# Nine plain tiles of the first expert group before the one-hot turns instead of seven, the other seven at 14 products a turn

## The reference, cut to what matters

```python
q = jnp.einsum('bsd,de->bse', xn, w_query).reshape(B, S, PEER_HEADS, 2, PEER_HALF)
s = jnp.einsum('bshpd,hpnd->bshpn', q, sub_keys)
top_s, top_i = lax.top_k(s, PEER_TOPK)
...
expert = i1 * PEER_N_KEYS + i2
gates = jax.nn.softmax(cand_s, axis=-1)
...
a = jax.nn.gelu(jnp.einsum('cd,ced->ce', xc, u), approximate=False) * gc
return jnp.einsum('ce,ced->cd', a, vv)
```

## Time and profile before

| | us |
|---|---|
| median of 3 runs | 3599.85 |
| lowest and highest run | 3598.56, 3603.22 |
| the profiled execution's own time | 3599.3 |
| its span, first to last instruction | 3597.6 |
| mean granted TensorE clock | 0.991 of full |
| TensorE busy | 3491.2 (97%) |
| VectorE busy | 2541.8 (71%) |
| ScalarE busy | 1731.0 (48%) |
| GpSimd busy | 116.1 (3%) |

### The profile page before, as it was taken

How to read it: one execution, slowest core, us unless ns; L and a number is a source line. 1 busy time by engine, 2 the same in 40 slices (tenths; PEclk the granted TensorE clock), 3 DMA queues, 4 the chain that set the end, 5 groups by cost and what they waited for, 6 DMA issues and landing times.

```text
span 3597.6 us, 70310 instructions
## 1 busy us (share of the span) xinstructions
PE 3491.2 (97%) x27342; PEld 3337.9 (93%) x27342; DVE 2541.8 (71%) x4337; ACT 1731.0 (48%) x3177; POOL 116.1 (3%) x209
## 2 busy tenths in 40 slices
PE   6899999999999999999999999999998999999998
PEld 6898889898899999999999999988966999999998
DVE  7976535888658797878787888943356776767555
ACT  4531113546855454545445445742155655555444
POOL 0001000000100000000000000000000000000000
PEclk9999999999999999999999999999999999999999
DMA  9979876654666868687877777532211455555554
GB/s 404 406 265 366 341 280 221 252 183 152 223 252 237 315 241 313 249 303 250 303 264 298 268 282 295 197 129 88 91 45 37 172 195 193 194 191 195 177 192 161
DMA packets 118196, 829.40 MB, mean 231 GB/s; under 512 B 13104, under 2 KB 13232, under 8 KB 26800
## 3 DMA queue, kind: packets, MB, share of 16 engines
q1 hardware_dynamic: 88416, 619.20, 47.5%
q0 software_dynamic: 29520, 206.58, 15.1%
HBM read 806.86 MB, written 16.78 MB: 229 GB/s over the span
## 4 chain that ended last, share of the span: by engine, by line
PE 88%; DVE 6%; ACT 2%; DMA 2%; issue 1%; POOL 0%; SPq 0%; DVEq 0%; ACTq 0%
PE ps L1182 23%; PE ps L1184 23%; PE ps L1183 23%; PE ps L1157 9%; DVE arena L1749 2%; PE ps L1265 1%; PE ps L1267 1%; PE ps L1268 1%; ACT arena L615 1%; DVE ring_low L1739 1%; DMA gates_scratch<-arena 1%; PE ps L1581 1%; DMA gates_scratch<-cb 1%; PE ps L1209 0%; PE ps L1211 0%
## 5 line engine op out<-in xcount | busy, mean ns | idle before, releaser
L615 ACT ACTIVATE w_parts<-ring 128x512 fp32r<-128x512 f32 x1288 | 791.7, 630 | 909.3 <-PE ps L1184 671.0
L1739 DVE TENSOR_TENSOR ring_low<-ring,w_parts 128x512 fp32r<-128x512 f32 x1288 | 831.6, 687 | 390.4 <-ACT w_parts L615 345.8
L1184 PE MATMUL ps<-x_high,ring_low 128*128 128x256 f32 (+1 forms) x3840 | 1081.2, 282 | 0.0
L1184 PEld LDWEIGHTS ps<-x_high,ring_low 128*128 128x128 f32 x3840 | 720.8, 188 | 7.7
L1182 PE MATMUL ps<-x_high,w_parts 128*128 128x256 f32 (+1 forms) x2464 | 701.8, 285 | 1.7 <-DVE ring_low L1739 1.0
L1183 PE MATMUL ps<-x_low,w_parts 128*128 128x256 f32 (+1 forms) x2464 | 700.6, 284 | 0.0
L1739 DVE TENSOR_TENSOR ring_low<-ring,w_parts_ff 128x512 fp32r<-128x512 f32 (+1 forms) x544 | 356.8, 674 | 197.8 <-ACT w_parts_ff L615 190.2
L1182 PE MATMUL ps<-at_high,w_parts 128*128 128x256 f32 x1792 | 494.6, 276 | 0.0
L1183 PE MATMUL ps<-at_low,w_parts 128*128 128x256 f32 x1792 | 494.6, 276 | 0.0
L1184 PE MATMUL ps<-at_high,ring_low 128*128 128x256 f32 x1792 | 494.6, 276 | 0.0
L615 ACT ACTIVATE w_parts_ff<-ring 128x512 fp32r<-128x512 f32 (+1 forms) x544 | 332.7, 619 | 317.2 <-PE ps L1184 254.5
(11 more groups left out here) (288 smaller groups left out, 6306.4 us busy)
## 6 DMA issues: line engine op xcount, KB each, us to landing
ada<-in_ada POOLq DMA_DIRECT2D x144, 1024.0 KB, 7.1
ring<-in_peer_down SPq DMA_DIRECT2D x128, 1024.0 KB, 4.9
ring<-in_peer_up SPq DMA_DIRECT2D x128, 1024.0 KB, 5.9
ring<-in_w_in SPq DMA_DIRECT2D x102, 1024.0 KB, 6.6
ring<-in_w_up SPq DMA_DIRECT2D x88, 1024.0 KB, 4.8
ring<-in_w_down SPq DMA_DIRECT2D x64, 704.0 KB, 4.0
arena<-in_ada SPq DMA_DIRECT2D x32, 1024.0 KB, 7.8
arena<-in_ada POOLq DMA_DIRECT2D x16, 1024.0 KB, 7.5
```

What stands on the lines that cost most here:

```text
L615: return nc.scalar.activation(*a, **k)
L1184: ins = mm(to, w_low, high(k), start=False, stop=(k == k_all - 1))
L1739: vv.tensor_tensor(ring_low[:, slot, cols], ring[:, slot, cols], parts[:, m, 0:w].bitcast(F32), ALU.subtract).then_inc(lo_ready, 1)
```

## The change

EARLY goes from 7 to 9. The first transposes (`turn_ids(0)`) come behind the fifth tile instead of the fourth, the second ones in the middle of the ninth. The remaining seven tiles, 112 products, are done two at a time in the first seven steps of each of the eight turns; a tile now runs across a turn's boundary, and none is left for the tail. A table gives the step at which ScalarE evicts each tile: steps 10, 19, 28, 37, 46 and 55 for tiles 9 to 14, two steps behind the tile's last product. Tile 15, whose last product lies at step 62, is evicted where it was. ScalarE evicts tile 7 before, and tile 8 behind, its copy of the second transposes, both ahead of the first gatings.

```diff
-EARLY = 7
+EARLY = 9
+AHEAD_TURN = 14
...
+HOLD_STEP = {u: 8 * (at // AHEAD_TURN) + at % AHEAD_TURN // 2 + 2
+             for u, at in ((u, 16 * (u - EARLY) + 14) for u in range(EARLY, 15))}
...
             hold(5)
             hold(6)
+            hold(7)
             turned(1)
+            hold(8)
...
-                        if n == 1 and i:
-                            hold(EARLY + i - 1)
+                        for u in range(EARLY, 15):
+                            if 8 * i + n == HOLD_STEP[u]:
+                                hold(u)
...
-            hold(14)
             for b in range(3):
                 high_of_first(b)
             hold(15)
...
-            for u in range(EARLY):
+            for u in range(EARLY - 1):
                 ahead(u)
-                if u == 3:
+                if u == 4:
                     turn_ids(0)
+            ahead(EARLY - 1, range(8))
             turn_ids(1)
+            ahead(EARLY - 1, range(8, KC))
             pe.wait_ge(ids_copied, 2)
...
-                    ahead(EARLY + i, range(2 * n, 2 * n + 2))
-            ahead(15)
+                    if n < 7:
+                        at = AHEAD_TURN * i + 2 * n
+                        ahead(EARLY + at // KC, range(at % KC, at % KC + 2))
```

## The result

| | before | after |
|---|---|---|
| median of 20 runs each, us | 3603.23 | 3608.62 |
| lowest and highest, us | 3598.11, 3608.04 | 3605.04, 3611.41 |
| ratio after to before | | 1.0016, 95% interval 1.0009 to 1.0023 |
| profiled execution, own time and span, us | 3599.3, 3597.6 | 3610.89, 3609.2 |

The change costs 5.4 us. This is a slowdown that twenty runs can tell, and it stays under the 0.2% that the prediction called no change. (The before kernel's median over twenty runs is 3.4 us above that of its first three, so the two numbers to compare are the forecast's +1.95 over 3599.85 and the +5.4 here.)

A forecast was written before the change was run, and what follows sets the result against it. ScalarE was taken to set the turns' pace: last copy +5.4, tail -3.4, hold(15) -0.4, clock +0.3, sum +1.9 on 3599.3, 3601.2; with 0.55 for the median 3601.8 us. Range 3595 to 3609.

The forecast's parts named there:

- ScalarE paces: Forecast's own case for the turns: ScalarE sets the pace, six stores late by about 1 us; chance 0.54.
- Two more tiles before the turns: Selection stretch: 13.9 us more TensorE work, through at 865.2, transposes at 836.5 and 861.3, at no cost.
- hold(8) ahead of the gatings: Start of the turns: waiting for the ninth tile's last product delays the first gating by 6.85 us.
- The turns: Gatings and copies: ScalarE's own work of 111.3 us sets the pace, against TensorE's 105.4.
- Store waits: Heads of blocks: six stores meet ring loads at 1.0 us each, 6 us, bounds 0 and 13.6; last copy +5.4.
- The tail: Last copy to first expert product: gate transfer takes 2.5 us instead of 5.9, so -3.4.
- hold(15): First expert stage: its product is ready early, so VectorE's 0.36 us wait goes, -0.4.
- The clock: Start of the expert stage: TensorE, idle some 8 us, starts at the lower clock; +0.3, bounds 0 and 1.8.
- nothing is won in the tail: Rival, tail: gate transfer still takes 5.9 us and the clock costs all of 1.8; +6.8, 3606.7 us, chance 0.08.
- stores set the pace: Rival, turns: ScalarE waits at each block's head for the store two blocks before; +9.5, 3609.4 us, chance 0.14.
- Stores in gaps: Rival, turns: ring loads fall in gaps, so no store wait; -4.1, 3595.8 us, chance 0.20.
- TensorE paces: Rival, turns: TensorE sets the pace, last one-hot at 972.3; -8.3, 3591.6 us, chance 0.04.

The follow-up runs named there:

- Latehold: Changed kernel with tile 8's eviction moved from ahead of the first gatings to behind the copy of step 1; median 3607.19 us, 1.0015 of the kernel before.
- after3: Changed kernel with a third stage buffer, so each store has a block more to land; median 3599.47 us, 0.9992 of the kernel before.
- Smallload: Changed kernel with nine ring loads cut to 64 KB each, output wrong; median 3600.24 us, 0.9995 of the kernel before.
- before3: Kernel before with a third stage buffer and nothing else; median 3602.46 us, 1.0002 of the kernel before.
- eight: Changed kernel with eight early tiles, 14 products a turn, one tile in the tail, two stage buffers; median 3600.65 us, 0.9999 of the kernel before.
- eight3: Changed kernel with eight early tiles, 14 products a turn, one tile in the tail and a third stage buffer; median 3594.55 us, 0.9981 of the kernel before.

## Why the prediction was right, and where its sum was off

The forecast was right in the bound (ScalarE paces), the sign and the size class. There is luck in the number: the median, 3608.62, lies 0.4 us inside the range's upper edge, and the profiled execution, 3610.89, outside it. Half of the 6.8 us between forecast and median is the base, 3.4 too low as a median of three runs, and the other half is the change itself, +5.4 for +1.95. The stage moved by +6.1 us where the sum said +1.9. Step by step, in the prediction's own terms:

*Two more tiles before the turns.* Right. TensorE was through at 865.0 (forecast 865.2), the transposes came at 836.55 and 861.05 (836.5, 861.3), and nothing waited for them that mattered.

*hold(8) ahead of the gatings.* Right: +6.7 us for the first gating, +6.85 forecast. Latehold shows 1.8 of it to be the eviction's place; the rest is the ninth tile itself.

*The turns.* Right. ScalarE's chain without its waits is 121.7 - 9.4 = 112.3 us (865.32 to 987.04), against 111.7; after3 measures it clean at 111.8. (The sum counts seven evictions of 0.27 between the first gating and the last copy; there are six.)

*Store waits.* **This is the term that was mis-sized**: "I take 1.0 a store", 6 us in all, came out as 9.4. The prediction had named the right stores: 7's, 15's, 43's and 51's are those with the waits of 3.11, 3.11, 2.31 and 0.71, and 27's has the last 0.18. The price of a meeting was wrong: 9.24 / 4 = 2.3 us for each of these four. It was taken near the median's 0.6, as that of a typical met store. But the eight stores under that median had their loads issued 0.6 to 2.7 us ahead, and the nearest of these, 0.6 ahead, took 8.1 us. Two of the four waits are at the upper bound, 3.1, which came from the worst row, 8.7: for a store that a load meets, that row was the nearer one. The Trainium skill's rule on round robin between queues ("DMA: Bandwidth & Descriptors", section "Queues, rings and completion order"), which the prediction set beside its sum and by which the stores "would lie nearer the upper bound", was the better guide. The trace agrees with it: a load issued 0.87 us behind a store still brought it to 9.0 us. Smallload shows the cause: without the loads' bytes 7.2 of the 9.4 go.

*The tail.* Right: -3.5 between the end of the last copy and the first expert product (9.45 before, 5.91 after), forecast -3.4. The gate transfer took 2.4 us (987.33 to 989.74), 2.5 forecast.

*hold(15).* Wrong, but small: VectorE still waits its 0.36 at 994.94. The prediction looked only at when the product is ready; the eviction stands behind `high_of_first(2)` in ScalarE's own order, at 994.45. The forecast of -0.4 fails on the order of one queue.

*The clock.* Sized low. The low clock lasts for 24 products, and the first 25 starts span 5.16 us (992.95 to 998.11); in the kernel before they span 4.48 (987.21 to 991.69), with the wait of 1.14 in them. From the first product to the end of the stage it is 98.28 us against 97.69, so clock and hold(15) together are +0.6 where -0.1 was forecast. The warning of the Trainium skill ("TensorE: Matmul & The Clock Gate", section "Why this matters for your kernels") held in direction; by it alone 1.8 was to be lost, and 0.6 was, because this stage used to wait 1.14 for a low part and does so no more.

Together: last copy +9.0 instead of +5.4 (against the first plain product), tail -3.5, behind it +0.6: +6.1. Of the miss of 4.2 the store waits make 3.4, and clock and hold(15) 0.7.

By number the forecast is not the nearest: "nothing is won in the tail" (+6.8) is closest to the +6.1 of the stage and the +5.4 of the medians, though its mechanism did not occur, and in absolute time "stores set the pace" (3609.4) is closest to 3608.62. The latter is also nearest by mechanism. Its condition was that the six met stores take some 7 us in the mean, and the ones behind steps 7, 15, 27, 35, 43 and 51 took 9.0, 9.0, 6.1, 5.7, 8.2 and 6.6, 7.4 in the mean. So by its own condition this rival had come about, at two thirds of its price. It and the forecast share one mechanism and differ in the price of a meeting, and the measured +6.1 lies about midway between their +1.9 and +9.5. The rival's price was too high, since two of the six still landed in time or nearly. "Stores in gaps", "TensorE paces" and "nothing is won in the tail" are all refuted by rows above.

Why does a change that fills two gaps of TensorE, and takes a tile out of the tail, lose? Between the first gating and the last copy the work of ScalarE is fixed, some 112 us. The two tiles added ahead delay its start by 6.7 (6.4 against the first plain product), and its chain grows from 119.1 to 121.7, since the late stores cost more than TensorE's quicker steps give back. Of TensorE's time freed in the turns and in the tail, only the 3.5 by which the last gate transfer is quicker come back. The kernel before could absorb late stores under TensorE's slower pace; the kernel after can't.

## What to carry to other kernels

Before work is moved off an engine that looks full, add up the work of the engine beside it between the same two points. If the two sums are within a few per cent of each other, the start of the second engine's chain is what counts, and work put ahead of that start costs what it delays it by (here 13.9 us of work delayed it by 6.7). Two transfers issued within about a microsecond of each other should each be priced by the slowest such pair in the trace and not by a median over wider distances; and where a buffer's refill waits for its store, a third buffer makes the order of the loads unimportant. An edit that gives nothing alone (before3, eight) can be half of one that gives 0.2% (eight3), because each uncovers the limit that the other removes.

## What the runs showed of the hardware that was not expected

Either order makes a store late, and the distance in time counts: a store issued 0.28 us behind a load took 8.2 us, and one issued 0.10 ahead of it 9.0, where stores alone mostly take 4.7. But one met 1.07 us behind its issue took only 6.6. This holds over all nine kernels here with full loads: the 28 stores with a ring load issued within 1.0 us of them (23 loads ahead of the store and 5 behind it) landed after 7.2 to 10.8 us, and the seven whose load came 1.07 to 1.58 behind after 5.6 to 6.8. The kernel before had one store of the first kind (8.1) and none of the second. In smallload two stores took 6.7 us with no large load near, which is not explained.

The length of TensorE's idle time did not alone decide its clock. In the kernel after, 2.57 us of idle brought it down (908.91: 1.83 us for eight entries, where 1.05 to 1.16 is usual, and a granted clock of 0.58 from 908.9 to 911.0), and so it did in nospread (975.57, granted clock 0.56 behind it). In eight the same 2.57 did not:

```profile
886.47 1.16 PE L1445 MATMUL ps<-arena 128*128 128x128 f32 x8 [2.57 <-ACT arena L620]
```

What else decides was not tried. And single runs of one kernel differ by some 6 to 10 us, more than this change is worth. The stage in the trace leaves out what scatters behind it, such as the 5.5 us above, and shows where a difference arises; but it is one execution, so a stage difference that the medians don't bear out, as latehold's, stays open.
